# Full attentions of a mixer encoder: probabilities scaled on GpSimd ahead of their transposes, outputs kept by channel

## The reference

```
def dense_attention(q, k, v):
    ...
    def attend(q_blk):
        logits = jnp.einsum("bqkgd,bskd->bkgqs", q_blk, k).astype(jnp.float32) * scale
        p = jax.nn.softmax(logits, axis=-1).astype(v.dtype)
        return jnp.einsum("bkgqs,bskd->bqkgd", p, v)
```

## Time and profile before

| | |
|---|---|
| time, median of 3 runs | 2740.06 us (2738.78 to 2741.49) |
| the profiled execution | 2739.07 us, its span 2737.3 us |
| mean granted TensorE clock | 0.996 |
| TensorE, products | 2652.6 us, 97% of the span |
| VectorE | 1286.7 us, 47% |
| ScalarE | 1007.7 us, 37% |
| GpSimd | 775.5 us, 28% |
| fold, line 1114 | 256 instructions (two for each of 128 products) |

### The profile page before, as it was taken

How to read it: one execution, slowest core, us unless ns; L and a number is a source line. 1 busy time by engine, 2 the same in 40 slices (tenths; PEclk the granted TensorE clock), 3 DMA queues, 4 the chain that set the end, 5 groups by cost and what they waited for, 6 DMA issues and landing times.

```text
span 2737.3 us, 36490 instructions
## 1 busy us (share of the span) xinstructions
PE 2652.6 (97%) x13956; PEld 2236.1 (82%) x13956; DVE 1286.7 (47%) x2668; ACT 1007.7 (37%) x2074; POOL 775.5 (28%) x534
## 2 busy tenths in 40 slices
PE   6999999999999999999999999999999999999998
PEld 4788878878888888878897887888888888888787
DVE  3575265722344355542346734675224443555323
ACT  3364114711344534521225631165124445354111
POOL 2310341024243342123422114200334342322232
PEclk9999999999999999999999999999999999999999
DMA  5100211011111231111420002100211213211122
GB/s 183 32 9 2 57 43 32 1 53 41 47 46 43 67 91 47 31 39 43 158 69 22 1 23 54 37 20 1 65 44 44 54 42 82 76 39 30 49 100 93
DMA packets 200376, 137.52 MB, mean 50 GB/s; under 512 B 20952, under 2 KB 186456, under 8 KB 200168
## 3 DMA queue, kind: packets, MB, share of 16 engines
q1 hardware_dynamic: 186380, 128.69, 16.6%
q10 hardware_dynamic: 13824, 6.49, 0.8%
HBM read 120.24 MB, written 19.10 MB: 51 GB/s over the span
## 4 chain that ended last, share of the span: by engine, by line
PE 90%; DVE 5%; ACT 2%; issue 1%; POOL 1%; DMA 0%; ACTq 0%; SPq 0%; POOLq 0%; DVEq 0%
PE ps L925 24%; PE ps L888 10%; PE ps L890 10%; PE ps L889 10%; PE ps L1126 4%; PE ps L1092 4%; PE ps L1076 4%; PE ps L988 3%; PE ps L990 3%; PE ps L989 3%; PE ps L1050 3%; PE ps L1051 3%; PE ps L1061 2%; PE ps L1053 1%; PE ps L1364 1%
## 5 line engine op out<-in xcount | busy, mean ns | idle before, releaser
L2199 POOL CAST wh<-wraw 128x1024 fp32r<-128x1024 f32 (+2 forms) x152 | 169.3, 1114 | 1625.7 <-PE ps L890 788.6
L888 PE MATMUL ps<-xh,wh 128*128 128x512 f32 x1088 | 426.7, 392 | 2.2 <-ACT pt_split L1630 2.2
L890 PE MATMUL ps<-xh,wl 128*128 128x512 f32 x1088 | 423.7, 389 | 0.0
L889 PE MATMUL ps<-xl,wh 128*128 128x512 f32 x1088 | 423.4, 389 | 0.0
L2201 POOL TENSOR_TENSOR wl<-wraw,wh 128x1024 fp32r<-128x1024 f32 (+2 forms) x152 | 401.0, 2638 | 12.2
L925 PE MATMUL ps<-xh,wh 128*128 128x512 f32 x896 | 366.4, 409 | 3.2 <-ACT att L1445 1.2
L925 PE MATMUL ps<-xh,wl 128*128 128x512 f32 x896 | 357.2, 399 | 0.0
L925 PE MATMUL ps<-xl,wh 128*128 128x512 f32 x896 | 356.4, 398 | 0.0
L1477 ACT ACTIVATE gs<-ps 128x512 f32<-128x512 f32 x96 | 57.0, 598 | 519.2 <-PE ps L890 514.7
L888 PEld LDWEIGHTS ps<-xh,wh 128*128 128x128 f32 x1088 | 204.3, 188 | 44.2 <-ACT pt_split L1630 3.0
L890 PEld LDWEIGHTS ps<-xh,wl 128*128 128x128 f32 x1088 | 204.2, 188 | 43.0
(11 more groups left out here) (279 smaller groups left out, 5057.9 us busy)
## 6 DMA issues: line engine op xcount, KB each, us to landing
wraw<-in_w_in_dram SPq DMA_DIRECT2D x128, 512.0 KB, 3.9
acc<-in_x_dram SPq DMA_DIRECT2D x16, 512.0 KB, 8.5
wraw<-in_w_branch_dram SPq DMA_DIRECT2D x64, 128.0 KB, 4.0
wraw<-in_w_out_dram SPq DMA_DIRECT2D x16, 512.0 KB, 3.5
dil_out<-cst ACTq DMA_DIRECT2D x96, 66.0 KB, 1.6
toep<-toep_row SPq DMA_DIRECT2D x16, 256.0 KB, 6.0
xres<-acc SPq DMA_DIRECT2D x8, 512.0 KB, 2.6
acc<-xres SPq DMA_DIRECT2D x8, 512.0 KB, 6.9
```

What stands on the lines that cost most here:

```text
L888: pe.matmul(dst, ah, bh, start=i == 0, stop=False)
L889: pe.matmul(dst, ah, bl, start=False, stop=False)
L890: last = pe.matmul(dst, al, bh, start=False, stop=i == len(ks) - 1)
L2199: inc(pool.tensor_copy(high, raw), w_hi[l])
```

## The change

Probabilities are divided by their row sum ahead of the transposes, and the outputs are never turned back to rows of tokens.

- VectorE: `sum_inverse(s - 1)` behind `maxima(s)`: the reciprocal of one row sum. `pair_outputs` and `gated` are gone in A and B. `pair_added` adds the two halves of a pair's product by channel: one from PSUM, the other as ScalarE has copied it to the same partitions.
- GpSimd: a new loop `dense_rows` beside the attention. It multiplies unit s-1's 128x1024 probabilities by the reciprocals in place (`rows_scaled`), splits queries in A, multiplies the added pair by the gate path into `gs`, and splits the next weight tiles in pieces (2 for a tile of B's tokens, 5 for each of two merge tiles). For the last pairs of a branch VectorE does the gating.
- TensorE: no fold, no transposes of `yn` in A and B. `transposes_part` waits for `rows_scaled` in place of `exp_done`.
- ScalarE: the pair's copy takes the 64 partitions of the other half alone. `split_high` waits for `pair_gated`.
- B's units now go in pairs of token blocks of one head, as A's did; `fold` is dropped; single semaphores are merged (`setup_done`, `gates_ahead`, `toep_stored`); counts of `pv_done` start with branch C (`values_done`). The list of loads on SP is written in two loops, in the same order.

```
 # plan and TensorE
-                for st in range(ST):
-                    for h in range(HEADS):
-                        kv = h // 2
-                        unit(bq_stack[:, h, st * P:(st + 1) * P], bk_stack[:, kv, 0, :], None,
...
+                for st, h in ((a + c, b) for a in range(0, ST, 2) for b in range(HEADS) for c in range(2)):
+                    kv = h // 2
+                    unit(bq_stack[:, h, st * P:(st + 1) * P], bk_stack[:, kv, 0, :], None,
...
                 def transposes_part(s, part):
-                    pe.wait_ge(exp_done[l], s + 1)
+                    pe.wait_ge(rows_scaled[l], s + 1)
                     g, chunks = units[s]["groups"][part]
...
                 def dense_attention(b):
                     u0, u1 = b["span"]
-                    y = iter(b["y"])
-                    for s, begun, paired, tiles_of in dense_steps(b):
-                        for st in tiles_of(s - 6):
-                            pe.wait_ge(o_freed_dve[l], units[s - 6]["o_count"])
-                            y_transposes(next(y), yn[:, st % 2, :])
+                    for s, begun, paired in dense_steps(b):
                         if begun(s):
                             if s == u0 + 1:
                                 pe.wait_ge(*freed(l, b["gate_fill"] + 3))
                             if s - 2 >= u0:
                                 pe.wait_ge(exp_done[l], s - 1)
                             logits(s)
-                        if paired(s - 4):
-
-                            pair = (s - 4) // 2
-                            pe.wait_ge(pair_emptied[l], pair + 1)
-                            for e, v in enumerate(pair_units(pair)):
-                                inc(pe.matmul(units[v]["o"], pair_out[:, pair % 2, e * P:(e + 1) * P],
-                                              fold[:, :], start=True, stop=True), pv_done[l])
                         if begun(s - 2):
                             transposes_part(s - 2, 1)
                         if paired(s - 3):
...
 # ScalarE
                             if paired(s - 3):
                                 pair = (s - 3) // 2
+                                own, other = product_rows(pair)
                                 act.wait_ge(pair_ready[l], pair + 1)
                                 if pair >= 2:
-                                    act.wait_ge(pv_done[l], 2 * pair - 2)
-                                inc(act.activation(pair_out[:, pair % 2, :], units[s - 3]["product"], ACT.Copy),
-                                    pair_emptied[l])
+                                    act.wait_ge(o_freed_dve[l], units[2 * pair - 3]["o_count"])
+                                inc(act.activation(pair_other[own, pair % 2, :], units[s - 3]["product"][other, :],
+                                                   ACT.Copy), pair_emptied[l])
...
 # VectorE
+                def sum_inverse(s):
+
+                    c = s % U_MAX
+                    dve.wait_ge(exp_done[l], s + 1)
+                    inc(dve.reciprocal(rs[:, c:c + 1], ssum[:, c:c + 1]), sums_set[l])
+
+                def pair_added(pair):
+
+                    own = product_rows(pair)[0]
+                    dve.wait_ge(pair_emptied[l], pair + 1)
+                    if pair >= 2:
+                        dve.wait_ge(pair_gated[l], pair - 1)
+                    inc(dve.tensor_tensor(yn[own, pair % 2, :], units[2 * pair]["product"][own, :],
+                                          pair_other[own, pair % 2, :], ALU.add), o_freed_dve[l], 2)
...
-                    for s, begun, paired, tiles_of in dense_steps(b) if n < 2 else []:
-                        if s == u1 + 5:
-                            y_rests(n, 0)
-                        for st in tiles_of(s - 6):
-                            gated(next(y), st)
+                    for s, begun, paired in dense_steps(b) if n < 2 else []:
                         if begun(s):
                             maxima(s, u0)
-                        if paired(s - 5):
-                            pair_outputs(s - 6)
+                        if begun(s - 1):
+                            sum_inverse(s - 1)
+                        if paired(s - 4):
+                            pair_added((s - 4) // 2)
                         if begun(s - 2):
                             rest_part(s - 2, 1)
                         if begun(s - 1):
                             rest_part(s - 1, 0)
+                    if n < 2:
+                        y_rests(n, 0)
...
 # GpSimd
+                def dense_rows(b, weights):
+
+                    for s, begun, paired in dense_steps(b):
+                        if b["n"] == 0 and paired(s) and s // 2 + A_RING < 2 * ST:
+                            queries(s // 2 + A_RING)
+                        if begun(s - 1):
+                            x, c = s - 1, (s - 1) % U_MAX
+                            pool.wait_ge(sums_set[l], x + 1)
+                            inc(pool.tensor_scalar(units[x]["prob"], units[x]["prob"], rs[:, c:c + 1], None, ALU.mult),
+                                rows_scaled[l])
+                        if paired(s - 4) and not gated_last((s - 4) // 2):
+                            pair = (s - 4) // 2
+                            own = product_rows(pair)[0]
+                            pool.wait_ge(o_freed_dve[l], units[s - 4]["o_count"])
+                            pool.wait_ge(rows_scaled[l], min(s, b["span"][1]))
+                            for dst, cols in product_places(pair):
+                                ins = pool.tensor_tensor(dst, dst, yn[own, pair % 2, cols], ALU.mult)
+                            inc(ins, pair_gated[l])
+                            pool.wait_ge(pair_gated[l], pair + 1)
+                        if s - b["span"][0] >= 3:
+                            next(weights, None)
...
+                    if t == tok_b[1]:
+                        dense_rows(branches[0], split_steps(t, 2))
+                    elif t == merge_b[0]:
+                        dense_rows(branches[1], itertools.chain(split_steps(t, 5), split_steps(t + 1, 5)))
+                    elif (l == 0 or t >= 2) and t != merge_b[1]:
                         split(t)
```

More of the change, by code:

```diff
@@ L16 @@
 from contextlib import ExitStack
+import itertools
 import numpy as np
@@ L222, in build @@
         ident = sb("ident", [P, P])
-        fold = sb("fold", [P, HD])
         gcol = sb("gcol", [P, KC + 3])
@@ L567, in dense_steps @@
             u0, u1 = b["span"]
-            at_once = 2 if b["n"] == 0 else 1
             def begun(s):
@@ L574, in paired @@
                 return u0 <= s < u1 and s % 2 == 1
-            def tiles_of(s):
-                count, more = divmod(s + 1 - u0, HEADS * at_once)
-                return range((count - 1) * at_once, count * at_once) if begun(s) and more == 0 else range(0)
-            for s in range(u0, u1 + 6):
-                yield s, begun, paired, tiles_of
+            for s in range(u0, u1 + 4):
+                yield s, begun, paired
         def plan_dense(b):
-            y = []
-            for s, begun, paired, tiles_of in dense_steps(b):
-                y += [tgroup("dve") for _ in tiles_of(s - 6)]
+            for s, begun, paired in dense_steps(b):
                 for part, x in ((1, s - 2), (0, s - 1)):
@@ L589, in plan_dense, with product_rows, product_places, gated_last @@
                         units[x]["groups"].append((tgroup("dve"), units[x]["chunks"][4 * part:4 * part + 4]))
-            return y
+            return []
+        def product_rows(pair):
+            h = units[2 * pair]["head"] % 2
+            return slice(h * HD, (h + 1) * HD), slice((1 - h) * HD, (2 - h) * HD)
+        def product_places(pair):
+            u = units[2 * pair]
+            own, c, t0 = product_rows(pair)[0], u["head"] // 2, u["st"] * P
+            if pair_units(pair)[0] == 2 * pair:
+                return [(gs[own, c, t0:t0 + 2 * P], slice(0, 2 * P))]
+            return [(gs[own, c, t0 + e * P:t0 + (e + 1) * P], slice((1 - e) * P, (2 - e) * P)) for e in range(2)]
+        def gated_last(pair):
+            return units[2 * pair]["st"] == ST - 2
         for b in branches:
@@ L710, in build, with values_done @@
         c_u1 = branches[2]["passes"][-1]["units"][1]
+        def values_done(s):
+            return s + 1 - c_u0
         pg_unit = [s for s, u in enumerate(units) if u["bias"] is not None for _ in u["groups"]]
@@ L817, in load_groups_outputs @@
                              dil_out[g, half * HALF:(half + 1) * HALF, :].rearrange("(t p) f -> p t f", p=P), dil_in[half])
-                for b in branches[:2]:
-                    for t in b["gate_tiles"] + (branches[1]["tok_tiles"] if b["n"] == 0 else []) + b["merge_tiles"]:
-                        load_tile(t)
+                for t in branches[0]["gate_tiles"] + branches[1]["tok_tiles"]:
+                    load_tile(t)
+                for t in branches[0]["merge_tiles"] + branches[1]["gate_tiles"] + branches[1]["merge_tiles"]:
```

(33 more changed lines are left out.)

77 lines of the change are left out of this document (35 added, 42 removed).

## The result

| | median | runs |
|---|---|---|
| before | 2739.73 us | 4 (2738.78 to 2741.49) |
| after | 3177.19 us | 4 (3174.77 to 3179.57) |

The changed kernel takes 1.160 times as long (95% interval 1.158 to 1.162), 437 us more. Forecast were 2900 us and a range from 2852 to 2960: the direction was right, the size was not.

What follows compares the result with a forecast made beforehand. TensorE, busy 97% of the span, was taken as the bound before, and a closed chain through GpSimd in each dense step after. 2739.07 + 130 (steps) + 3 (query splits) + 28 (clock) = 2900 us, range 2852 to 2960.

Steps and rivals of the forecast that it cites:

- The step that failed: GpSimd's multiplication of 128x1024 probabilities in each dense step of A and B, taken as 1.07 us.
- the four ends: Behind the last maximum of each dense attention: 1.6 us longer, less folds and yn transposes, net -0.7 us each.
- the scaling is slow: GpSimd's multiplication takes 1.50 us, giving 2953 us, or 2.46 us, giving 3072 us; chance 0.09.
- The round: Dense steps: logits, maximum, reciprocal, scaling, transposes, next logits in a closed chain, 4.57 us in A, 4.38 in B.
- some 250 us: Expected TensorE idle time before the transposes in four dense stages, less what the values fill, released by GpSimd's scaling.
- The clock: TensorE's granted clock falls in odd dense steps, 1.5 us each in A, 1.1 in B, once in three pairs: 28 us.
- a fall in every pair: Rival: TensorE's clock falls in each pair of dense steps, costing 83 us, 2955 us in all; chance 0.08.
- 130: Microseconds added in two layers by longer dense steps: +30.0 in A, +36.2 in B, -1.4 at the ends, per layer.
- The 3 us of query splits: GpSimd's query splits in A's odd steps delay the scaling by 0 to 0.25 us on 12 steps a layer.
- What hides: GpSimd's gating and cut weight splits stand behind the scaling with 3 us until the next; nobody waits for them.
- Contention: GpSimd slowed beside VectorE in dense steps: expected not to occur; otherwise 5.0 us a step in A, 53 us more.
- The other side: Rival: dense steps form no closed chain, TensorE keeps the removed work, about 45 us, so 2695 us; chance 0.04.

Runs made afterwards that it cites:

- one_column: Changed kernel with GpSimd scaling one column of the 1024, all waits kept and the other columns left undivided: 2791.27 us.
- filler_both: Changed kernel with unread 512-column products on TensorE ahead of the transposes, 14 in odd and 8 in even steps: 3108.16 us.
- no_scaling: Changed kernel without the division by row sums, transposes waiting for the exponential alone, GpSimd copying one column: 2733.17 us, 0.998 of the kernel before.

## Why the prediction was wrong

**The step that failed** is the size of one term: "The scaling itself is nowhere in the trace. The nearest row is GpSimd's one-input pass over 128x1024, 1.07 us; the other bound is its two-input pass over the same columns, 2.46 us. I take 1.07, since a multiplication by one number for each partition streams one tensor." It measured 2.84 us, 1.77 more, and above both bounds: a cast and a two-tensor pass were no bracket for a third operation, and that it streams one tensor said nothing of its time. Over 30 rounds in each of four attentions that is 120 x 1.77 = 212 us, and 7 in the four ends. The rival "the scaling is slow" had the right mechanism and 0.09 of the chance; its 3072 at 2.46 us still lies too low.

**The round** was right as a mechanism and in its other terms. With 2.84 for the 1.07 the prediction's own sum gives 1.2 + 30 x 6.34 = 191.4 us for A and 1.2 + 30 x 6.15 = 185.7 for B; with the clock held there were 193.3 and 188.5. `one_column` confirms it from the other side. The expected idle time ahead of the transposes, "some 250 us", came as 348.

**The clock** was right in kind and too small: "The gap found before a fall and the gap in the loop are so near each other that I take one fall in three pairs: 28 us." The price of a fall was right, up to 1.6 us in A and 0.9 in B for the 1.5 and 1.1 that it took; the count was not: with a scaling that is 1.77 us longer, the gap without a product is 3.8 us and the clock falls in nearly every pair. Its cost, 69 us by `filler_both`, stands near the 83 that the prediction had for a fall in every pair. No run has a scaling of 1.07 us; with 0.29 on GpSimd the clock held (0.994), with 0.75 on VectorE it did not (0.966), so how often it would have fallen at 1.07 stays open. By the page that the prediction cites, the Trainium skill's "TensorE: Matmul & The Clock Gate", Part 1, TensorE is throttled unless recent activity releases it. The trace agrees: behind 3.80 us without a product the granted clock was 0.52.

**Together**: 2739 + 130 + 219 (the scaling's term) + 3 + 69 (the clock) = 3160, 17 us under the median and 19.5 under the profiled execution. Of these, the rounds with the clock held are 10.5 us longer in four attentions than the sum has them (1.9 in A and 2.8 in B of layer 1, 0.06 to 0.09 a round). The stretches outside them are 13.2 us longer than before where the sum has 4.3 for the four ends (7.1 of scaling less 4 x 0.7), so 8.9 more; no run takes these apart. The 3 us of query splits were not found: in the changed kernel's rows a split ends at 184.55 + 0.72 = 185.27 and the scaling starts at 185.36, no later behind its reciprocal than in the step without them. In their place the low clock makes 74 us in the attentions of the profiled executions (838.6 against 764.7 with the clock held), not 69.

**What hides**: the gating, the split queries and the cut weight splits cost little, as the prediction had it. No run leaves them out, but `one_column` has them all, and its steps are within 0.1 us of what the round and TensorE's own work give. **Contention** with VectorE did not come, as the prediction had it: the scaling's 128 rows lie between 2842 and 2852 ns.

**The other side.** Its price, "about 45 us", for what is removed from TensorE was too high even without any scaling: `no_scaling` kept 7 us, since the pair's addition had been put ahead of the odd step's subtractions. The prediction passed over it: "VectorE and ScalarE have slack in a pair, so those are worth nothing by themselves." Slack over a pair is not slack at each place in it. In its better place 33 us are kept; where the other 12 of the 45 are isn't shown.

## What to carry to other kernels

An operation that has no row is not bounded by rows of other operations on the same engine; where a forecast hangs on it 124 times, it wants a row of its own, and the range has to reach beyond its neighbours. Once a round is longer than TensorE's own step, work on another engine inside it costs its whole length in each step, and here once more by the clock that falls in the gap; a division that commutes with the product belongs behind it, where it meets 64x256 numbers for a pair instead of twice 128x1024. When work is moved between steps of different load, ask what stands behind it in that very step: 0.43 us of VectorE cost 26 us more in the odd step than in the even one.

## What the runs showed of the hardware

GpSimd's multiplication of 128x1024 float32 in place by one number for each partition takes 2.84 us as a tensor_scalar (0.29 us and 2.5 ns for each further column; 2.77 with the constant 1.0) and 1.89 us as a tensor_tensor with a repeated column, though a cast of that size takes 1.07 and a tensor_tensor of two full tensors 2.46, these two from one tensor into another. VectorE does the same tensor_scalar in 0.75 us. Why the form with fewer operands is the slower one isn't shown by any run. And adding unread products to TensorE's wait made the kernel faster, 3177 to 3108 us, with the granted clock back from 0.939 to 0.995.
